# Second feed-forward: seven block products in place of eight for the value projection, weight sums on GpSimd, downs between a pair's up-projections

## The reference, cut to what matters

```python
def conv_ffn(x, prev, w_up, conv_w, conv_b, w_down):     # x: tokens x 1024, w_up: 1024 x 5632
    up = x @ w_up
    u, val = up[..., :D_FF], up[..., D_FF:]               # D_FF = 2816
    u_pad = concatenate([prev, u], axis=1)
    c = conv_b + sum(conv_w[j] * u_pad[:, j:j + L] for j in range(3))
    h = gelu(c, approximate=True) * val
    return h @ w_down, u_pad[:, -2:]
```

## Time and profile before

| what | us |
|---|---|
| median of 3 runs (2579.36 to 2583.35) | 2583.18 |
| the profiled execution's own time | 2581.35 |
| its span, first to last instruction | 2579.5 |
| TensorE busy | 2452.5 (95%) |
| VectorE, ScalarE, GpSimd busy | 1614.0, 1149.6, 44.0 |
| pass f=2, from u of tile 2 to u of tile 20 | 304.5 |
| pass f=3, from u of tile 2 to u of tile 20 | 335.1 |

### The profile page before, as it was taken

The page is one execution under the profiler, slowest core; times in us unless marked ns, Lnnn a source line. Parts: engine busy times, 40 slices in busy tenths (PEclk is TensorE's granted clock), DMA queues, the critical chain, the costliest instruction groups (busy, mean ns, idle before and its releaser), DMA issues. The chain is left out here.

```text
span 2579.5 us, 37702 instructions
## 1 busy us (share of the span) xinstructions
PE 2452.5 (95%) x15399; PEld 2142.2 (83%) x15399; DVE 1614.0 (63%) x2922; ACT 1149.6 (45%) x1822; POOL 44.0 (2%) x66
## 2 busy tenths in 40 slices
PE   7999999989999999999998999889999999999997
PEld 4777988877888889999996677767788889999996
DVE  5667576675765556665656655665766556655556
ACT  4655454554343334343336666664344333423333
POOL 0000000000000000000000000000000000000000
PEclk9999999999999999999999999989999999999998
DMA  4222223323433322422323242222332323332322
GB/s 159 66 67 90 82 85 102 125 100 96 153 104 123 102 90 92 138 82 90 109 77 106 83 130 63 80 75 83 111 131 92 104 92 98 99 116 82 97 85 97
DMA packets 83592, 255.18 MB, mean 99 GB/s; under 512 B 12963, under 2 KB 30540, under 8 KB 81484
## 3 DMA queue, kind: packets, MB, share of 16 engines
q1 hardware_dynamic: 64348, 202.45, 25.0%
q0 software_dynamic: 5792, 28.05, 3.4%
q10 hardware_dynamic: 13280, 22.28, 2.6%
HBM read 225.93 MB, written 26.74 MB: 98 GB/s over the span
## 5 line engine op out<-in xcount | busy, mean ns | idle before, releaser
L447 PE MATMUL banks<-act_hi,w_lo 128*128 128x272 f32 (+1 forms) x2952 | 973.4, 330 | 15.7 <-DVE act_lo L2301 6.7
L447 PE MATMUL banks<-act_hi,w_hi 128*128 128x272 f32 (+1 forms) x2952 | 960.2, 325 | 0.0
L447 PE MATMUL banks<-act_lo,w_hi 128*128 128x272 f32 (+1 forms) x2952 | 958.3, 325 | 0.0
L425 ACT ACTIVATE w_hi<-w_raw 128x1024 fp32r<-128x1024 f32 x366 | 380.8, 1055 | 690.8 <-PE banks L470 487.2
L430 DVE TENSOR_TENSOR w_lo<-w_raw,w_hi 128x1024 fp32r<-128x1024 f32 x366 | 442.9, 1222 | 365.4 <-ACT w_hi L425 365.0
L447 PEld LDWEIGHTS banks<-act_hi,w_lo 128*128 128x128 f32 x2952 | 558.7, 189 | 75.4 <-issue 20.6
L447 PEld LDWEIGHTS banks<-act_lo,w_hi 128*128 128x128 f32 x2952 | 559.4, 190 | 43.2 <-issue 1.7
L447 PEld LDWEIGHTS banks<-act_hi,w_hi 128*128 128x128 f32 x2952 | 558.2, 189 | 43.8
L482 DVE TENSOR_TENSOR acc<-acc,banks 128x272 f32<-128x272 f32 (+1 forms) x624 | 314.7, 518 | 190.8 <-PE banks L470 187.3
L470 PE MATMUL banks<-h_hi,w_lo 128*128 128x272 f32 (+1 forms) x1056 | 345.3, 327 | 22.2 <-DVE acc L482 12.8
L470 PE MATMUL banks<-h_hi,w_hi 128*128 128x272 f32 (+1 forms) x1056 | 343.4, 325 | 0.0
(11 more groups left out here) (242 smaller groups left out, 2581.2 us busy)
## 6 DMA issues: line engine op xcount, KB each, us to landing
w_raw<-wall SPq DMA_DIRECT2D x366, 512.0 KB, 3.6
normed<-h_scratch POOLq DMA_DIRECT2D x20, 352.0 KB, 4.2
h_scratch<-acc POOLq DMA_DIRECT2D x3, 2176.0 KB, 7.8
h_scratch<-acc POOLq DMA_DIRECT2D x3, 2048.0 KB, 7.6
gstates<-state ACTq DMA_DIRECT2D x4, 1024.0 KB, 6.4
gla_s<-gstates ACTq DMA_DIRECT2D x4, 1024.0 KB, 6.8
bias<-bias_scratch ACTq DMA_DIRECT2D x28, 128.0 KB, 2.6
bias_scratch<-bias_rows ACTq DMA_DIRECT2D x8, 383.0 KB
```

The lines of the kernel that those rows point to most:

```text
L425: nc.scalar.activation(WH[:, b % RING], WR[:, b % RAW], ACT.Copy).then_inc(w_hi, 1)
L447: last = nc.tensor.matmul(PS[:, bank, 0:n], w, a[X][:, k, o:o + n], start=(k == 0 and first), stop=(k == KT - 1 and w is wh and a is AH))
```

## The change

For pairs g = 1 to 10 of passes 2 and 3, the value projection of both tiles of the pair is one product of 2x2 blocks (two tiles of hidden channels, two halves of the 1024 inputs, two halves of the tokens). It is made of seven block products (after Strassen and Winograd) in place of eight. A block product is 4 blocks of weights by 256 or 272 tokens, 12 matmuls. The sums of activations and of weights that this needs are made on the chip:

- GpSimd makes, once per pass, four sums lo+hi of activations and four differences (8 instructions of 128x1024 or 128x1088), and for each pair four sums of weights of 128x512, three of them after both raw blocks have landed.
- ScalarE rounds the four activation sums once per pass (`sums_hi`, in tile 2), VectorE makes their rests (`sums_lo`, two in tile 2 and two in tile 3).
- The blocks of a pair in `weight_order` are now u, d, d, u, va, vs, vb, v4: eight roundings, v4 of half size, of which vs and v4 are sums and not loaded, in place of six.
- TensorE: u(t), downs(g-1), u(t+1), then the seven products. Product results go to banks 0 to 3. The u of the next pair waits for the reading of product 6 (`vp_read`).
- ScalarE copies the first product, VectorE combines the others by seven additions or subtractions of 256 or 272 columns from PSUM (`read_products`), and then multiplies by gelu(c) out of SBUF (`times`).
- On VectorE in an even tile the entries of the norm table stand after `conv` and ahead of the additions of the downs. The new tables `DVE_SEVEN` and `ACT_SEVEN` move some entries: s0, s1, a0 in tile 4; s2, s3, a2 in 6; F0 in 8; F1 in 10; n0 in 12; n1 in 14.
- Some semaphores outside the feed-forward are merged (`one` in place of `tb_one` and `sn`), with the same order.

```diff
@@ weight_order
+    def ffn_tile_pair(f, g):
+        for what in ("va", "vs", "vb", "v4"):
+            put((what, f, g), w0 + 4 + 6 * (g - 1) + 1)
@@ w_load
+            if r >= RAW:
+                before = LOADED[r - RAW]
+                sp.wait_ge(w_lo, before + 1)
+                if names[before][0] == "vb":
+                    sp.wait_ge(v_sum, 4 * SEVENS[names[before][1:]])
@@ w_round
+                if names[b][0] in ("va", "vs"):
+                    act.wait_ge(v_sum, 4 * SEVENS[names[b][1:]] - 1)
+                elif names[b][0] == "v4":
+                    act.wait_ge(v_sum, 4 * SEVENS[names[b][1:]])
@@ pe_ffn_tile
+            if t % 2 == 0 and seven(f, t // 2 - 1):
+                pe.wait_ge(vp_read, 8 * SEVENS[f, t // 2 - 1] - 1)
+            elif t == 0 and seven(f - 1, FG - 1):
+                pe.wait_ge(vp_read, 8 * SEVENS[f - 1, FG - 1])
+                pe.wait_ge(h_made, TILE[f - 1, FT - 1, len(CHUNKS[1 - X]) - 1])
...
+            if seven(f, t // 2):
+                if t % 2:
+                    pe_products(pe, f, t // 2)
+                return
+        def pe_products(pe, f, g):
...
+            product("va", 1, own(AH, 0, 0), own(AL, 0, 0), 2)
+            pe.wait_ge(t_lo, 4 * SEVEN.index(f) + 4)
+            product("va", 0, made(TH, 0), made(TL, 0), 3)
+            product("vs", 1, made(TH, 1), made(TL, 1), 0)
+            product("vs", 0, made(TH, 2), made(TL, 2), 1)
+            product("vb", 1, own(AH, 1, 0), own(AL, 1, 0), 2)
+            product("vb", 0, made(TH, 3), made(TL, 3), 0)
+            product("v4", 0, own(AH, 1, 1), own(AL, 1, 1), 3)
@@ dve_ffn
+            def seven_tile(f, t):
+                g = t // 2
+                if t % 2 == 0:
+                    rest_after(dve, ("u", f, t))
+                    conv(f, t)
+                    steps = ffn_steps((DVE_FFN[0], DVE_SEVEN[0]), f, t)
+                    if g == 1:
+                        for i in range(2):
+                            sums_lo(f, i)
+                    for step in steps:
+                        dve_step(dve, *step)
+                    dve_ffn_adds(dve, f, g - 1)
+                    for x in range(2):
+                        rest_after(dve, ("d", f, g - 1, x))
+                    return
...
+                early, even, odd_tile = read_products(f, g)
+                rest_after(dve, ("u", f, t))
+                conv(f, t)
+                rest_after(dve, ("va", f, g))
+                early()
+                rest_after(dve, ("vs", f, g))
+                even()
+                odd_tile()
+                rest_after(dve, ("vb", f, g))
+                dve_ffn_lo(dve, f, t - 1)
+                rest_after(dve, ("v4", f, g))
+                dve_ffn_lo(dve, f, t)
@@ act_ffn
+            def seven_tile(f, t):
+                g = t // 2
+                bias(f, t)
+                for step in ffn_steps((ACT_FFN[0], ACT_SEVEN[0]), f, t):
+                    act_step(act, *step, 6)
...
+                if t % 2 == 0:
+                    if g == 1:
+                        sums_hi(f)
+                    gelu(f, t)
+                    act_ffn_downs_done(act, f, g - 1)
+                    return
...
@@ gpsimd
+                    gp_act_sums(gp, f)
+                    for g in range(1, FG):
+                        gp_three_sums(gp, f, g)
+                        if g == 2:
+                            h_load(gp, i, X, 2)
+                        gp_fourth_sum(gp, f, g)
+                        if g == 2:
+                            h_load(gp, i, X, 3)
+                        if g == 3 and i < 4:
+                            h_store(gp, i, X)
```

More of the change, by code:

```diff
@@ L72, with seven @@
 KV_TILE = 13
+SEVEN = (2, 3)
+def seven(f, g):
+    return f in SEVEN and g >= 1
 def weight_order():
@@ L412, in build @@
         TILE = tally([(f, t, c) for f in range(4) for t in range(FT) for c in range(len(CHUNKS[f % 2]))])
+        VALS = tally([(f, t, c) for f in range(4) for t in range(FT) if not seven(f, t // 2) for c in range(len(CHUNKS[f % 2]))])
+        SEVENS = tally([(f, g) for f in range(4) for g in range(FG) if seven(f, g)])
+        LOADED = [b for b in range(NW) if names[b][0] not in ("vs", "v4")]
+        RAWI = {b: r for r, b in enumerate(LOADED)}
         AQ = tally([(X, p, c) for X in range(2) for p in range(8) for c in range(len(CHUNKS[X]))])
@@ L1483, in dve_ffn @@
             for f, t in ffn_tiles(l):
-                for step in ffn_steps(DVE_FFN[0], f, t):
+                if seven(f, t // 2):
+                    seven_tile(f, t)
+                    continue
+                for step in ffn_steps((DVE_FFN[0], DVE_SEVEN[0]), f, t):
                     dve_step(dve, *step)
@@ L1496, in dve_ffn @@
                         rest_after(dve, ("kv", 0, x))
-                for step in ffn_steps(DVE_FFN[1], f, t):
+                for step in ffn_steps((DVE_FFN[1], DVE_SEVEN[1]), f, t):
                     dve_step(dve, *step)
@@ L1559, in act_ffn @@
                     bias_rows(t - 3)
-                for step in ffn_steps(ACT_FFN[0], f, t):
+                for step in ffn_steps((ACT_FFN[0], ACT_SEVEN[0]), f, t):
                     act_step(act, *step, 6)
@@ L2419, in _ @@
             for i, X in PASSES[1:]:
-                for y in range(4):
+                f = {(3, 1): 2, (4, 0): 3}.get((i, X))
+                for y in range(2):
                     h_load(gp, i, X, y)
-                if i < 4:
+                if f is None:
+                    for y in range(2, 4):
+                        h_load(gp, i, X, y)
+                else:
+                    gp_act_sums(gp, f)
[8 more added lines that the diff above has]
+                            h_store(gp, i, X)
+                if f is None:
                     h_store(gp, i, X)
```

243 lines of the change are left out of this document (217 added, 26 removed).

## The result

The changed kernel takes 2704.8 us (median of 4 runs, 2700.39 to 2711.18) against 2583.14 of the kernel before on the same chip: ratio 1.0477, 95% interval 1.0453 to 1.05. It is slower by 122 us; I had forecast 50 slower, with a range that ended at 2662.

The account below looks back on a forecast made before the run. TensorE, busy 95%, was taken as the bound. Terms -26.9 + 33 - 8 + 17.5 + 13.3 + 4.4 + 2.5 + 14.5 = +50.3 us on 2581.35 gave 2631, forecast 2620 to 2643 (chance 0.50), range 2601 to 2662.

Parts of the forecast that it names:

- Matmuls removed: Value projection, ten pairs in each of f=2 and f=3: 84 matmuls for 96-matmul work, 26.9 us less (bounds 20.9 to 29.1).
- what hangs on the odd tile: VectorE's 5.2 us after the last product fits under u's 5.6 or 6.0; with pass change and end, +2.5 us.
- Downs moved ahead, f=3: Even tiles: downs' fifth unit waits for VectorE's first addition, 3.3 us per pair, 33 us; today's stall goes, 8; net +25.
- pass f=2 has no stall by itself: Downs' fifth unit, due at 5.4 us after u's copy, could go on at 5.1: 0.3 us of slack.
- I take it as hidden: GpSimd's weight sums, with up to 3.8 us each for two of them, counted as costing nothing.
- rival 4: GpSimd becomes the bound: above 3.8 us per weight sum, f=2 pairs lose twice the excess; 2655 at 5 us; chance 0.07.
- rival 2: VectorE and GpSimd hinder each other, a convolution tap held in each of twenty pairs: 17 us more, 2649; chance 0.15.
- my sum of waits: TensorE's wait terms in the forecast: +33, -8, +17.5, +13.3, +4.4 and +2.5 us.
- up to 2.5 each is hidden: GpSimd's eight 1024-column activation sums, tiles 1 and 2 of f=2; beyond that 8 us per us, once; estimated 2.2 each.
- Norm work: Between convolution and additions in even tiles, stalling TensorE: 17.5 us in f=2, 13.3 in f=3 (tiles 2, 4, 6).
- Clock: TensorE's clock falls after new gaps: five long at 1.7 us, half of ten shorter at 1.2; +14.5 (bounds 0 and 25).
- rival 1: Clock doesn't fall at gaps of about 3 us and costs little after longer ones: about 36 us slower, 2617; chance 0.18.

Follow-up runs that it names:

- e3: Changed kernel, even-tile downs' additions ahead of norm work, and GpSimd weight sums from each pass's second pair cut to 8 of 512 columns: 2643.62 us.
- e9: Kernel before, eight products, only the downs moved between u and val in even tiles of f=2 and f=3, on all engines and in weight order: 2633.62 us.
- e5: Changed kernel with each GpSimd addition replaced by a memset of the same region, writing but reading nothing: 2648.17 us.
- e4: Changed kernel with unread matmuls ahead of the downs' fifth unit, in f=3 and in tiles 4, 6, 10, 12, 14 of f=2: 2678.04 us.
- e11: e9 plus four GpSimd 128x512 additions per pair, pairs 1 to 10 of f=2 and f=3, on a buffer nobody reads: 2653.71 us.
- e8: e6 with weight and activation sums on VectorE (activation sums in tiles 2, 3), seven products from each pass's third pair, GpSimd computing nothing: 2604.64 us.
- e14: e9 with VectorE's additions ahead of norm work, four ahead of the convolution in f=3, and ScalarE's norm work behind the downs: 2594.65 us.
- e6: Changed kernel, even-tile additions ahead of norm work, and in f=3 four of them ahead of the convolution: 2641.89 us.

## Why the prediction was wrong

The direction was right and the size was not: +50 forecast, +122 measured.

- **Matmuls removed: right.** Matmuls of 256 columns are 0.12 apart, as taken:

```profile
2181.18 0.28 PE L1490 MATMUL banks<-act_hi,w_lo 128*128 128x256 f32 x1
2181.30 0.29 PE L1490 MATMUL banks<-act_lo,w_hi 128*128 128x256 f32 x1
2181.42 0.28 PE L1490 MATMUL banks<-act_hi,w_hi 128*128 128x256 f32 x1
```

From the odd tile's copy of u to the next even tile's are 15.5 us in f=2, which is the matmuls and nothing else (84 of val in 9.95, 24 of u in 5.57), and 16.6 in f=3 by the same sum, from tile 6 to the end. So the cover of "what hangs on the odd tile" held, but for tiles 4 and 12 of f=2 (18.0 each) and tile 4 of f=3 (20.0). Its 5.2 us come to 5.0 by the terms that I gave, which changes nothing.

- **Downs moved ahead, f=3: right.** I said a stall of 3.2 of which 3.0 shows as a gap. e3 and e9 have 3.0 in every even tile without norm work. That pass f=2 has no stall by itself was right within 0.8 us a tile (tiles 16, 18, 20: 17.4 to 17.6 between the copies of u, 16.8 of matmuls, and 16.8 in e3).

- **"I take it as hidden": the step that failed.** In the sum GpSimd's work costs nothing. I asked whether GpSimd would be done in time. With the weight sums it was: an addition takes 1.27 to 1.3 us when not held, a third of the limit in rival 4. What I did not put into the sum is that VectorE stands still meanwhile. That was rival 2, at 0.15, and its mechanism is what the rows show; but I let it act on one tap per pair, 17 us in all. It acts on whatever VectorE wants next, in f=3 on up to two copies of two elements (2.2 us in four of the seven pairs without norm work), in f=2 on the scalings. e5 gives its size: where GpSimd only writes, TensorE waits 61 us more than before (78.5 and 17.4), and my sum of waits was 63; in the changed kernel it waits 111 more (128.2). So the wait terms were about right for a GpSimd that holds nobody up, and the term that I put at nothing was worth some 50 us of waits. That memsets are also shorter than additions was not taken apart. The Trainium skill, "SBUF — State Buffer", section "Who interferes with whom", gives the rule for a VectorE instruction with two SBUF inputs. The trace agrees for the scalings and folds, and e5 for its other half, that GpSimd must read SBUF. The same section says more, which I had read over: a VectorE copy can enter a mode that takes both ports, and then it contends with GpSimd's writes too. The traces are in line with this, though no row names the mode. In the changed kernel the copy of two elements was held for an addition, and in e5, where GpSimd only writes, it was longer at times, by less than a memset of 512 elements (0.53), while the two-input instruction above kept its length. All copies of that line in one stretch of e5 (number, then shortest, median and longest in ns):

```profile
L1573 DVE COPY u<-halo x6: 159/286/582, 2435.9 to 2534.5; 128x2 f32<-128x2 f32 x6
```

- **Activation sums "up to 2.5 each is hidden": wrong.** They took 2.4 to 3.4 each in pass f=2 (2.5 to 3.5 in f=3), and 23 us in all beside VectorE. The start of pass f=2 lost 13.1 and 4.8 us in two gaps, where I had 8.4 (4.4 over the 4.0 of before); in e5 the two are 5.9 and 1.4.

- **Norm work: mis-sized.** I had stalls of 3.9, 3.9, 1.8, 2.6, 2.6, 2.6 in tiles 4 to 14 of f=2, 17.4 us. The gaps are 6.1, 6.3, 2.3, 5.1, 5.0, 5.1, sum 29.9. The order was as I read it; the instructions in it were longer, by 2 us in tile 4, since they ran beside GpSimd (4.87 for 2.87). In e5 the same six gaps add to 14.3. In f=3, where I had norm work on top of the fifth unit's stall, tiles 2, 4 and 6 have 10.0, 9.0 and 10.0, and 8.0, 6.8 and 7.0 in e5. So this miss too is GpSimd's.

- **Clock: mis-sized.** I let five long gaps and half of the short ones fall, 14.5 us, with 25 as the bound. In e9 the gaps of 3.0 us in f=3 behind which I looked, seven, are all followed by 0.57 to 0.58, at 1.6 us each; rival 1 is refuted, though two of the ten gaps of 3.0 us in e3 kept 1.00. Filled gaps give back 27 us (e4), and what the waits don't explain in the profiled run is 43. I had taken one gap of 3.13 us near the end, with a fast matmul behind it, for half the new ones. There the clock did stay at 1.00; behind the same gap in e9, 3.14 us at 2597.19, it was 0.50 for 4 us. So one gap is no rule, and one matmul is no sign: in e9 the first three matmuls behind a gap of 3.02 are fast as well, and the half-speed spacing begins with the fifth.

Together, in the profiled run: matmuls -27 (said -27), waits of TensorE about +113 (said +63), the low clock +43 (said +14.5; the 43 is a remainder, of which e4 shows 27). Beyond the 50 of GpSimd's holds I can't split the 113 cleanly by place: e9 to e11 put the move at 52 us (clock included) and additions of 512 columns, at a mild place, at 20 on top; what is left belongs to additions at worse places, to the activation sums and to norm steps in other tiles, which e3, e5 and e8 took away several at a time.

## What to carry to other kernels

Before an operation is moved, list what stands ahead of the instruction that frees its resource on every other engine: the old order hid 5.6 us of VectorE's list behind val, and the move uncovered it in every pair. An idle GpSimd was no free engine beside a busy VectorE here; four additions that VectorE does in 0.7 us each were better put into its own list. And a gap of 3 us in TensorE cost about 4.6 in e9, so it is better split or filled.

## What was not expected of the hardware

- How small the held instruction may be: a copy of two elements, 1.24 us for 0.16. A memset of 1024 elements on GpSimd leaves a two-input subtraction on VectorE at 1.23.
- GpSimd's additions are held in return: 1.62 and 1.82 us for 512 elements where others take 1.27, and 2.3 in some.
- The granted clock was 0.57 in the 4 us behind a gap of 3.02 us and 1.00 in the 3.7 us after those, but a gap of 3.13 at the end of the kernel before left it at 1.00. Gaps of 1.02 us left it at 1.00 in the whole pass (e14). Between them it goes both ways: the gaps of pass f=3 in e6 are 2.1 to 2.3 us, and it fell behind four of the ten and stayed behind six. Two stretches behind such gaps (2.10 and 2.09 us):

```profile
2349.09:2353.09 4.00, 4.00 (x20) 4.00 (x21) 1.92 (x6) 0.00 (x0) 0.87 (x1) 0.58 0.00 0
2425.48:2429.48 4.00, 4.00 (x32) 4.00 (x33) 2.74 (x7) 0.00 (x0) 0.87 (x1) 1.00 0.02 4
```
